# Query and key norms unit by unit in the second block, and four state-space input units as seven block products

## What is computed

```python
h = rms_norm(x, norm1_g)
proj = h @ w_in
z, xbc, dt_raw, q, k, v, g_ssd, g_att = jnp.split(proj, IN_SPLITS, axis=-1)
...
xbc = lax.conv_general_dilated(xbc, conv_w, ...) + conv_b     # four taps along the tokens
xbc = jax.nn.silu(xbc)
...
q = rms_norm(q.reshape(b, s, ATT_N_HEADS, HD), q_norm_g)      # 16 heads of 64
k = rms_norm(k.reshape(b, s, KV, HD), k_norm_g)               # 4 heads of 64
q = partial_rope(q, cos, sin)                                 # turns the first 16 of 64 columns
k = partial_rope(k, cos, sin)
...
scores = jnp.einsum('bnqhgd,bnkhd->bnhgqk', qb, kk) * ATT_SCALE
```

## Time and profile before

| | us |
|---|---|
| median of three runs | 1435.3 |
| the profiled execution, its own time | 1434.83 |
| span of the profiled execution | 1433.1 |
| PE busy in the span | 1364.2 |
| att2 units 1 to 5 on PE | 595.6 to 627.4 |
| xbc units 8 to 11 with the transposes on PE | 627.4 to 660.0 |
| attention on PE, with its xbc and z units | 660.0 to 749 |
| experts, from the first expert product | 995 to 1433 |

### The profile page before, as it was taken

How to read it: one execution, slowest core, us unless ns; L and a number is a source line. 1 busy time by engine, 2 the same in 40 slices (tenths; PEclk the granted TensorE clock), 3 DMA queues, 4 the chain that set the end, 5 groups by cost and what they waited for, 6 DMA issues and landing times.

```text
span 1433.1 us, 27506 instructions
## 1 busy us (share of the span) xinstructions
PE 1364.2 (95%) x11344; PEld 1156.5 (81%) x11344; DVE 736.6 (51%) x1664; ACT 324.6 (23%) x732; POOL 403.1 (28%) x318
## 2 busy tenths in 40 slices
PE   7999999999999999999999999999999998888877
PEld 6978999998899999998888999998666665555555
DVE  4838675341588895668844664544333322222122
ACT  1143311331111101112555540102111111111110
POOL 1516651530288887330001234830000000000000
PEclk9999999999999999999999999999999999999899
DMA  9443534224444435444433443389999999999997
GB/s 350 141 153 142 183 116 164 91 91 158 157 158 174 149 128 216 155 163 162 144 121 133 151 158 135 137 336 397 415 424 425 426 424 426 424 426 426 426 426 321
DMA packets 60843, 349.39 MB, mean 244 GB/s; under 512 B 12872, under 2 KB 13992, under 8 KB 22192
## 3 DMA queue, kind: packets, MB, share of 16 engines
q1 hardware_dynamic: 57408, 339.13, 60.7%
q10 hardware_dynamic: 2960, 6.40, 1.3%
q0 software_dynamic: 352, 2.11, 0.4%
HBM read 396.43 MB, written 1.51 MB: 278 GB/s over the span
## 4 chain that ended last, share of the span: by engine, by line
PE 85%; DMA 6%; DVE 4%; issue 3%; ACT 1%; POOL 1%; SPq 1%; DVEq 0%; ACTq 0%; POOLq 0%
PE bank L583 21%; PE bank L504 15%; PE bank L1385 9%; PE bank L1408 5%; PE bank L1433 5%; PE bank L1038 4%; PE bank L1419 4%; PE bank L518 4%; PE bank L1236 3%; DMA work<-w_down_e_dram 3%; DMA con_sb<-w_down_e_dram 2%; PE bank L631 2%; PE bank L765 1%; PE bank L721 1%; DMA hT<-w_up_e_dram 1%
## 5 line engine op out<-in xcount | busy, mean ns | idle before, releaser
L2272 DVE TENSOR_TENSOR xT<-xT,bank 128x512 f32<-128x512 f32 (+2 forms) x102 | 64.7, 640 | 231.3 <-PE bank L1408 186.9
L504 PE MATMUL bank<-work,ring 128*128 128x256 f32 x704 | 153.6, 379 | 0.0
L1385 PE MATMUL bank<-work 128*32 128x256 f32 x1056 | 133.5, 397 | 18.6 <-issue 10.8
L504 PEld LDWEIGHTS bank<-work,ring 128*128 128x128 f32 x704 | 133.4, 190 | 18.8 <-issue 1.0
L583 PE MATMUL bank<-hT,ring 128*128 128x128 f32 x832 | 103.4, 276 | 1.3 <-DVE work L2263 1.2
L1385 PEld LDWEIGHTS bank<-work 128*32 128x32 f32 x1056 | 67.4, 114 | 45.8 <-issue 26.7
L583 PEld LDWEIGHTS bank<-hT,ring 128*128 128x128 f32 x832 | 98.0, 192 | 6.5 <-issue 4.4
L504 PE MATMUL bank<-hT,ring 128*128 128x256 f32 x384 | 85.0, 380 | 1.3 <-DVE work L2263 1.3
L1385 PE MATMUL bank<-ring,work 128*32 128x256 f32 x528 | 75.2, 407 | 9.4 <-issue 7.0
L1408 PEld LDWEIGHTS bank<-selw,work 128*128 128x128 f32 x320 | 57.5, 189 | 30.8 <-issue 24.6
L504 PEld LDWEIGHTS bank<-hT,ring 128*128 128x128 f32 x384 | 72.1, 190 | 11.4 <-issue 2.0
(11 more groups left out here) (475 smaller groups left out, 3051.4 us busy)
## 6 DMA issues: line engine op xcount, KB each, us to landing
work<-w_up_e_dram SPq DMA_DIRECT2D x32, 1024.0 KB, 26.4
work<-w_gate_e_dram SPq DMA_DIRECT2D x31, 1024.0 KB, 26.0
work<-w_down_e_dram SPq DMA_DIRECT2D x28, 1024.0 KB, 26.9
ring<-w_up_dram SPq DMA_DIRECT2D x22, 1024.0 KB, 4.9
ring<-w_down_e_dram SPq DMA_DIRECT2D x21, 1024.0 KB, 26.0
ring<-w_gates_dram SPq DMA_DIRECT2D x20, 1024.0 KB, 4.9
ring<-w_gate_e_dram SPq DMA_DIRECT2D x18, 1024.0 KB, 26.8
ring<-w_up_e_dram SPq DMA_DIRECT2D x15, 1024.0 KB, 26.6
```

What stands on the lines that cost most here:

```text
L504: m = mm(b[:, j * SEQ:(j + 1) * SEQ], w[:, k, j * P:(j + 1) * P], tile(k), start=(k == 0), stop=(k == kt - 1))
L1385: m = mm(b[j * CAP:(j + 1) * CAP, 0:HIDDEN], xg[:, k, j * CAP:(j + 1) * CAP], w[:, k, :], start=(k == 0), stop=(k == KD - 1), tile_positio ...
L2272: return v.tensor_tensor(dst, a, b, ALU.add)
```

## The change

Three things change, all between the first att2 unit and the end of the attention.

1. `xbc` units 8, 9, 10 and 11 become seven-product units, in one list with the att2 units (`SEVEN_IN2`). Each now takes three banks instead of one, POOL makes four sums for each, DVE makes a second set of four mixes (from `hT`) and the additions of each before its convolution, and ACT copies each "one".
2. Squares, their sums, roots, scaling, gains and turning are done in parts: ACT squares each of units 0 to 4 as soon as it has copied it (two buffers `qk_sq` instead of one), DVE sums each, and the queries (`scaled_heads`, `gained_heads`, `turned_heads` of heads 0 to 15) are finished ahead of the additions of att2 unit 5, the keys behind them.
3. The eight scalings of `xT` move behind the attention on DVE.

The core of the diff (PE's wait values and the DVE bodies that only got ranges of heads are cut):

```diff
-        qk_sq = area(19456, TT, QK_HEADS * A_DIM)
+        qk_sq = [area(8192 + 512 * n, TT, 256) for n in range(2)]
...
-        SEVEN_ATT2 = [1, 2, 3, 4, 5]
+        SEVEN_IN2 = [("w_att2", i) for i in (1, 2, 3, 4, 5)] + [("w_xbc2", i) for i in (8, 9, 10, 11)]
...
+            def seven_xbc(i):
+
+                seven("in2", None, SEVEN_IN2, in2("w_xbc2", i), hT, xbc_mix, att_sums, mixed=4)
+
             for i in (8, 9, 10):
-                to_features(("xbc", i), "w_xbc2", hT)
+                seven_xbc(i)
...
-            to_features(("xbc", 11), "w_xbc2", hT)
+            seven_xbc(11)
...
-            weight_sums("att2", "w_att2", SEVEN_ATT2, att_sums)
+            weight_sums("in2", None, SEVEN_IN2, att_sums)
...
+            unit_squares(0)
             for i in range(1, 6):
                 if i < 5:
-                    kept("att2", SEVEN_ATT2, i, gates2_kept)
+                    kept("in2", SEVEN_IN2, i, gates2_kept)
                 att_kept(i)
+                if i < 5:
+                    unit_squares(i)
+                if i == 3:
+                    qk_roots(4, 0, A_HEADS)
+                if i == 4:
+                    qk_roots(5, A_HEADS, QK_HEADS)
+            kept("in2", SEVEN_IN2, in2("w_xbc2", 8), gates2_kept)
...
-            att_joined(2)
-            for k in range(KD):
-                stt(xT[:, k, :], xT[:, k, :], col("norm_final", k), rs[:, 0, 0:SEQ])
-                if k == KD // 2 - 1:
-                    att_joined(3)
-            att_joined(4)
-            att_joined(5)
...
+            first_mixes("in2", hT, xbc_mix, 4)
+            att_joined(2)
+            last_mixes("in2", hT, xbc_mix, 4)
+            for i in (0, 1):
+                unit_sums(i)
+            att_joined(3)
+            for i in (2, 3):
+                unit_sums(i)
+            scaled_heads(0, A_HEADS)
+            att_joined(4)
+            dve.wait_ge(S("sines"), nth("sines"))
+            gained_heads(0, A_HEADS, "q_gain")
+            unit_sums(4)
+            turned_heads(0, A_HEADS)
+            att_joined(5)
+            scaled_heads(A_HEADS, QK_HEADS)
+            gained_heads(A_HEADS, QK_HEADS, "k_gain")
+            turned_heads(A_HEADS, QK_HEADS)
...
             for i in (8, 9, 10, 11):
+                xbc_joined(i)
                 conv_xbc(i)
...
             attention("swa", A_HEADS, ATT_SCALE, "swa_mask", True, sc2, fill_xbc)
+            for k in range(KD):
+                stt(xT[:, k, :], xT[:, k, :], col("norm_final", k), rs[:, 0, 0:SEQ])
```

More of the change, by code:

```diff
@@ L400, in build @@
                       block4(scratch[:, 2560:3072])]
-        SEVEN_ATT2 = [1, 2, 3, 4, 5]
+        SEVEN_IN2 = [("w_att2", i) for i in (1, 2, 3, 4, 5)] + [("w_xbc2", i) for i in (8, 9, 10, 11)]
+        in2 = lambda w_name, i: SEVEN_IN2.index((w_name, i))
+        xbc_key = lambda i: ("in2", ("w_xbc2", i), "b") if ("w_xbc2", i) in SEVEN_IN2 else ("xbc", i)
+        xbc_mix = [block4(area(9216 + 512 * n, 512)) for n in range(4)]
         att_mix = [block4(spare[:, 512 * n:512 * n + 512]) for n in range(4)]
@@ L573, in half_unit, with seven @@
                 unit_read()
-            def seven(name, w_name, units, n, src, mix, sums, by_token=False):
+            def seven(name, w_name, units, n, src, mix, sums, by_token=False, mixed=0):
                 i, x = units[n], x_blocks(src)
@@ L1077, in _ @@
                 else:
-                    seven("att2", "w_att2", SEVEN_ATT2, i - 1, gainT, att_mix, att_sums, by_token=True)
+                    seven("in2", None, SEVEN_IN2, in2("w_att2", i), gainT, att_mix, att_sums, by_token=True)
                 if i == 0:
@@ L2035, in att_kept @@
             def att_kept(i):
-                key = ("att2", i, "b") if i else ("att2", 0)
+                key = ("in2", ("w_att2", i), "b") if i else ("att2", 0)
                 act.wait_ge(product_ready, made(*key))
@@ L2057, in _, with unit_squares, qk_roots @@
             A_(dt_e, dt_e, ACT.Ln, bias=ones[:, 0:1]).then_inc(S("softplus_out"), 1)
+            def unit_squares(i):
+                key = ("in2", ("w_att2", i), "b") if i else ("att2", 0)
+                act.wait_ge(bank_free(*key), used(*key))
+                if i >= 2:
+                    act.wait_ge(S("qk_sums"), i - 1)
+                A_(qk_sq[i % 2], qkv_tok[:, :, i * 256:(i + 1) * 256], ACT.Square)\
+                    .then_inc(S("qk_squares"), 1)
+            def qk_roots(sums, h0, h1):
+                act.wait_ge(S("qk_sums"), sums)
+                A_(by_tile(qk_r)[:, :, h0:h1], by_tile(qk_ss)[:, :, h0:h1], ACT.Ln, bias=eps, scale=1.0 / A_DIM)\
+                    .then_inc(S("act_step"), 1)
+                act.wait_ge(S("act_step"), nth("act_step"))
+                A_(by_tile(qk_r)[:, :, h0:h1], by_tile(qk_r)[:, :, h0:h1], ACT.Exp, scale=-0.5).then_inc(S("qk_root"), 1)
+            unit_squares(0)
             for i in range(1, 6):
                 if i < 5:
-                    kept("att2", SEVEN_ATT2, i, gates2_kept)
+                    kept("in2", SEVEN_IN2, i, gates2_kept)
                 att_kept(i)
[L2062 to L2068, removed]
+                if i < 5:
[5 more added lines that the diff above has]
+            kept("in2", SEVEN_IN2, in2("w_xbc2", 8), gates2_kept)
             act.wait_ge(product_ready, made("acum"))
@@ L2815, in att_joined @@
             def att_joined(i):
-                uppers("att2", SEVEN_ATT2, i - 1, gates2_kept)
-                joined("att2", SEVEN_ATT2, i - 1, gates2_kept)
+                uppers("in2", SEVEN_IN2, in2("w_att2", i), gates2_kept)
+                joined("in2", SEVEN_IN2, in2("w_att2", i), gates2_kept)
             att_joined(1)
@@ new lines, in unit_sums, with scaled_heads @@
+            def unit_sums(i):
+                dve.wait_ge(S("qk_squares"), i + 1)
+                v.tensor_reduce(by_tile(qk_ss)[:, :, 4 * i:4 * i + 4],
+                                qk_sq[i % 2].rearrange("p t (h d) -> p t h d", d=A_DIM), AX.X, ALU.add)\
+                    .then_inc(S("qk_sums"), 1)
+            def scaled_heads(h0, h1):
+                dve.wait_ge(S("qk_root"), nth("qk_root"))
+                for t in range(TT):
+                    w = heads_of(t, h0, h1)
+                    m = mul(w, w, b3(qk_r[:, t * QK_HEADS + h0:t * QK_HEADS + h1], h1 - h0, A_DIM))
+                m.then_inc(S("dve_step"), 1)
+                dve.wait_ge(S("dve_step"), nth("dve_step"))
```

90 lines of the change are left out of this document (44 added, 46 removed).

## The result

The changed kernel takes 1441.66 us (median of six executions, 1440.07 to 1442.48) where the kernel before, timed beside it, takes 1435.92: a ratio of 1.0034, with a 95% interval of 1.0023 to 1.0045. It is slower by 4.9 us by the ratio and by 5.7 by the medians; the forecast was 1440.7. (One of the six executions of the kernel before was disturbed and took 1917.7 us: it counts in the median, which is 1435.75 without it, and not in the ratio.)

The account below looks back on a forecast made before the run. PE bounds the kernel (busy 95%, 85% of the chain); POOL makes DVE's chain 11.2 us late, so PE's waits outweigh its 4.0 gain: 5.4 later, 1440.2, plus 0.5 for the median, 1440.7; range 1431 to 1446.

Parts of the forecast that it names:

- bank "b": xbc 9's bank is that of att2 unit 5, free after DVE's additions and ACT's copy: 642.2, wanted by PE at 636.3.
- wait at xbc 10: PE, at bank "b" of xbc 10 at 648.5, waits 1.8 us for the convolution of xbc 8, ending at 650.3.
- The turn-taking: Between 607 and 639, DVE operations with two SBUF inputs alternate with POOL's sums, each losing 0.95 to 1.0 us.
- The four losses: DVE waits for POOL: mixes 1.8 us remaining, scalings 2.1, gains 1.7, turnings 5.6; 11.2 late at att2 unit 5's additions.
- the part without interference: DVE's chain from 607.1 without POOL: additions of att2 unit 5 end at 630.4, convolution of xbc 8 at 639.4.
- POOL's stretched sums: POOL, held by DVE's long operations, makes PE about 1.1 us late in xbc 8.
- the low clock: PE's slow return after 5.9 us idle: at most 1.4 us, falling into the following 1.8 us wait, so nothing.
- `xT` in its new place: Eight scalings at 0.4 us behind the attention cost nothing, standing in an idle stretch of 17.92 us.
- A port kept by a train: Rival: DVE operations without a semaphore between go through together; about 6 of 11.2 us less lost, 1435.9; chance 0.10.
- The keys met no sum: Against a rival: sums for xbc 10 come first, four to five short key operations lose 1.0 each, 1445 to 1446; chance 0.07.
- The faster rival: Cover holds: POOL waits come to under 2.1 us at the convolution of xbc 8, PE keeps 4.0, 1431.3; chance 0.13.
- the 4.0: PE's most possible gain in us: 2.6 from four units at 6.25 for 6.91, plus the 1.32 gap before xbc 11.

Follow-up runs that it names:

- the quiet version: Changed kernel with only xbc unit 10 by seven products, its sums after xbc 8, queries' scaling after POOL's last att2 sum: 1433.63 us, ratio 0.9979 to the kernel before.
- e5_norms_alone: Kernel before plus norms unit by unit and xT scalings behind the attention, xbc 8 to 11 plain: 1436.3 us for 1437.69, ratio 0.9994.

## Why the prediction was right

The sign, the place and the size came out. Point by point, each time counted from the begin of the stretch (the prediction's times less 602.33, those of after less 599.65):

| point | predicted | measured |
|---|---|---|
| additions of att2 unit 5 end | 39.0 | 39.6 |
| bank "b" free for xbc 9 | 39.9 | 40.6 |
| idle PE before it | 5.9 | 5.20 |
| keys done (`q_tok2`) | 42.7 | 43.6 |
| convolution of xbc 8 ends | 48.0 | 49.0 |
| wait at xbc 10 | 1.8 | none |
| wait at xbc 11 | 0.7 | 0.70 |
| first transpose of weights | 71.7 | 73.1 |

**The turn-taking** held, and the short operations with POOL busy took 1.24 to 1.35 us. The four losses came to the forecast total but not as forecast one by one: the scalings 2.2 (forecast 2.1) and the gains 1.5 (1.7), against the quiet version's rows; the turning 6.7 (5.6): six of its twelve operations waited out a sum, as forecast, but lost 0.96 to 1.08 us each, and a seventh lost 0.36; the mixes 0.75, their own time included (1.8), as the scaling began 17.69 us into the stretch (617.34) and 16.94 in the kernel without them (e5_norms_alone, 619.43). The sum is 11.1 for 11.2, and that it is so near is luck: the turning was taken 1.1 too low and the mixes 1.05 too high. What made the additions 0.6 late was the part without interference, taken a little too short. To count one lost us for each meeting was right only because DVE still had operations when POOL made its last sum; the version with `xT` in its old place shows where the count fails. Nor did every operation meet a sum before that: four of the eight products and the last addition of the turning took 0.28 us, in short pauses of POOL's list or behind its end.

**PE's side** had two misses that left the end where it was. POOL's stretched sums held PE 2.3 us, not 1.1: 1.1 in the att2 units (xbc 8 begins 26.19 us into the stretch, 25.09 before) and 1.2 in xbc 8 (7.44 us to its end, 6.26 with the short sums). So its idle time was 5.20 and not 5.9. Where the prediction had a wait of 1.8 at xbc 10 there was none, because the low clock took 2.4 us of the same time (7.84 for 5.46 in six products), more than the 1.4 I had set as its most. The prediction said that it would fall into that wait and cost nothing; keeping PE busy showed the cost to be nothing, to 0.01 us of the stretch. But 2.4 is more than the wait had room for (1.8 forecast, 1.95 with PE kept busy): that nothing was left over is owed to the second wait, at xbc 11, and so is luck in part.

**The 1.4 us missing** in the stretch (73.1 for 71.7) are thus 1.0 of the chain at the convolution of xbc 8, 0.6 of it from the additions and 0.4 from the keys and additions behind (9.4 us between the two points for 9.0), and 0.4 behind it. They came to PE by DVE's list, which has no idle time from there to the convolution of xbc 10, and by the wait of 0.70 at xbc 11, not by the long wait in xbc 9.

**`xT` in its new place** was free: the eight take 3.25 us at 740.21, and DVE still stands idle 14.75 us after them, for 17.92 before.

**The rivals.** A port kept by a train would have let the four last operations of the turning through together; the first three waited one by one. The keys met no sum in the changed kernel, thanks to PE's own wait: with that wait removed they did (3.99 for 0.91). The faster rival's price was not reached: with the added sums made short the stretch is 0.8 us shorter, not 4.0, as PE came 1.1 late to xbc 8 and two convolutions held it for 0.89 and 0.86. The times of that version say 0.19% (0.10 to 0.28), not the 0.3% of 1431.3. As the scalings and the mixes still met the sums for the att2 units there, it stays open whether PE would gain the 4.0 with no meeting at all, as the prediction said.

## What to carry to other kernels

Before giving POOL more work, count the operations with two SBUF inputs that DVE has in the same stretch. In this case, while both lists lasted and POOL's had no pause, each of the short ones waited out about one whole POOL operation (1.24 to 1.35 us for 0.28), so many short ones are the worst neighbours; and the total loss was set by the list that ended first, POOL's. Lay POOL's work beside DVE operations that read PSUM, and merge short operations. A wait that is seen on PE may be the mildest place for a late chain: look at what the next reader of that chain would wait for before moving work to remove it.

## What the runs showed of the hardware

The clock fell more readily than I had thought. Behind 5.20 us of idle PE 16 matmuls took 3.45 us instead of 1.95 to 2.05, and in the version with merged turnings it happened behind an idle time of 2.60 (granted clock 0.72 over the six us from 638). Behind 1.95 us, in the version that kept PE busy, it did not: the products went on at 1.95 for 16, and the clock stayed at 1.00. A longer idle time did not always cost more: the 16 matmuls at the same place behind it took 3.33 us after 2.60 idle, 2.94 after 8.65 (`xT` back), 3.26 after 10.07 (additions of unit 5 first) and 3.62 after 15.00 (seven products alone). That the engines take turns was expected; that the total lost stays nearly the same when operations are put in front (10.8 for 10.4 us) was not.

Two inputs in SBUF are not the whole rule. The small operation of rows 8 is a TENSOR_SCALAR with one input, and took 0.96 us beside a POOL sum, where one of the same size took 0.19 at 991.0 in the same trace; a TENSOR_REDUCE with one input of 512 columns took its 0.69 us beside POOL (627.57 in the changed kernel) as without it (628.54 in e5_norms_alone). Which operations with one input wait, no run here separates.
